# Memory staged by 32 partitions and turned by VectorE, and three quarters of the residual turned through a DRAM scratch issued by ScalarE

## The reference

```python
h = rms_norm(x, norm_mix)
proj = h @ w_in                       # 2048 x 3904: latents of q and kv, rope key, q, k, v of the second head group
q  = rms_norm(c_q,  norm_q_lat)  @ w_q_b
kv = rms_norm(c_kv, norm_kv_lat) @ w_kv_b
o_mla = mla_attention(...)            # 8 heads, causal softmax
o_sb  = stick_breaking_attention(...) # 8 heads
mixed = concatenate([rms_norm(o_mla, norm_mla_out), rms_norm(o_sb, norm_sb_out)])
x = x + mixed @ w_out                 # 2048 x 2048
mem_n = rms_norm(mem, norm_mem_src)
x = x + memory_cross_attention(rms_norm(x, norm_mem_x), mem_n, w_mem_q, w_mem_kv, w_mem_o)
x = x + hierarchical_moe(rms_norm(x, norm_ffn), ...)   # 32 experts, 12 MB of weights each, top 2 of 8 in one of 4 groups
return rms_norm(x, norm_final)
```

## Time and profile before

| | us |
|---|---|
| median of the three runs | 1350.66 |
| lowest and highest | 1350.59, 1352.66 |
| the profiled execution | 1350.58 |
| span of its profile | 1348.8 |
| PE busy in the span | 992.5 |
| DVE busy | 576.0 |
| ACT busy | 303.9 |
| POOL busy | 40.9 |
| bytes moved by DMA | 486.40 MB |

### The profile page before, as it was taken

The page is one execution under the profiler, slowest core; times in us unless marked ns, Lnnn a source line. Parts: engine busy times, 40 slices in busy tenths (PEclk is TensorE's granted clock), DMA queues, the critical chain, the costliest instruction groups (busy, mean ns, idle before and its releaser), DMA issues.

```text
span 1348.8 us, 20643 instructions
## 1 busy us (share of the span) xinstructions
PE 992.5 (74%) x8516; PEld 595.7 (44%) x8516; DVE 576.0 (43%) x1132; ACT 303.9 (23%) x537; POOL 40.9 (3%) x92
## 2 busy tenths in 40 slices
PE   8999999999999975666555666655566655566656
PEld 7888898888888522222222222212222222222222
DVE  5555567776656643233322233332223332223324
ACT  5554457774544100000000000000000000000002
POOL 1300000130000000000000000000000000000001
PEclk9999999999999997778777778787787787777878
DMA  7777764447869999999999999999999999999997
GB/s 245 262 243 250 214 176 125 152 150 276 290 235 354 359 432 429 434 431 432 430 432 434 430 430 430 434 431 430 430 435 431 431 431 431 434 431 430 430 427 307
DMA packets 78021, 486.40 MB, mean 361 GB/s; under 512 B 9944, under 2 KB 25438, under 8 KB 64799
## 3 DMA queue, kind: packets, MB, share of 16 engines
q1 hardware_dynamic: 77484, 483.46, 89.0%
q10 hardware_dynamic: 306, 2.11, 0.4%
q0 software_dynamic: 192, 0.31, 0.2%
HBM read 481.14 MB, written 4.72 MB: 360 GB/s over the span
## 4 chain that ended last, share of the span: by engine, by line
PE 50%; DMA 46%; SPq 1%; DVE 1%; issue 1%; ACT 0%; DVEq 0%; ACTq 0%
DMA gu<-in_w_up 42%; PE ps L1053 10%; PE ps L606 8%; PE ps L608 8%; PE ps L607 8%; PE ps L1108 5%; DMA down<-in_w_down 4%; PE ps L1032 2%; PE ps L1065 1%; PE ps L586 1%; PE ps L851 1%; PE ps L852 1%; PE ps L853 1%; PE ps L778 1%; SPq L471 0%
## 5 line engine op out<-in xcount | busy, mean ns | idle before, releaser
L1053 PE MATMUL ps<-gu,xe 128*32 128x256 f32 x3968 | 284.9, 450 | 305.8 <-DMA gu<-in_w_up 305.3
L2144 DVE TENSOR_TENSOR x_sum<-ps,x_sum 128x512 f32<-128x512 f32 x240 | 149.1, 684 | 508.3 <-PE ps L1065 508.3
L1053 PEld LDWEIGHTS ps<-gu,xe 128*32 128x32 f32 x3968 | 139.7, 129 | 468.9 <-DMA gu<-in_w_up 328.5
L1619 DVE TENSOR_TENSOR w_lo<-w_raw,w_hi 128x1024 fp32r<-128x1024 f32 (+1 forms) x137 | 164.6, 1207 | 117.7 <-ACT w_hi L1226 114.2
L606 PE MATMUL ps<-w_hi,a_hi 128*128 128x512 f32 (+1 forms) x468 | 183.3, 392 | 0.0
L607 PE MATMUL ps<-w_lo,a_hi 128*128 128x512 f32 (+1 forms) x468 | 179.8, 384 | 0.0
L608 PE MATMUL ps<-w_hi,a_lo 128*128 128x512 f32 (+1 forms) x460 | 176.8, 384 | 0.0
L1226 ACT ACTIVATE w_hi<-w_raw 128x1024 fp32r<-128x1024 f32 (+1 forms) x137 | 141.9, 1040 | 128.7 <-PE ps L608 98.2
L1538 ACT ACTIVATE sg<-ps 128x128 f32<-128x128 f32 x31 | 8.6, 278 | 654.3 <-PE ps L1053 654.3
L1108 PE MATMUL ps<-down,act_t 128*32 128x512 f32 x976 | 112.4, 601 | 6.1 <-DMA down<-in_w_down 6.1
L607 PEld LDWEIGHTS ps<-w_lo,a_hi 128*128 128x128 f32 x468 | 88.0, 188 | 16.4
(11 more groups left out here) (335 smaller groups left out, 831.6 us busy)
## 6 DMA issues: line engine op xcount, KB each, us to landing
down<-in_w_down SPq DMA_DIRECT2D x29, 4096.0 KB, 22.7
gu<-in_w_gate SPq DMA_DIRECT2D x28, 4096.0 KB, 31.7
gu<-in_w_up SPq DMA_DIRECT2D x28, 4096.0 KB, 40.9
w_raw<-in_w_in SPq DMA_DIRECT2D x56, 512.0 KB, 5.1
w_raw<-in_w_out SPq DMA_DIRECT2D x32, 512.0 KB, 4.4
gu<-in_w_up SPq DMA_DIRECT2D x18, 512.0 KB, 6.1
w_raw<-in_w_mem_kv SPq DMA_DIRECT2D x16, 512.0 KB, 3.5
down<-in_w_down SPq DMA_DIRECT2D x13, 512.0 KB, 15.2
```

The source lines that it names most:

```text
L1053: mm = pe.matmul(ps[5][j * SLOTS:(j + 1) * SLOTS, 0:2 * P].rearrange("s (m f) -> s m f", m=2), xe[:, k, :], gu[side][:, :, k, j * P:(j + 1 ...
L1619: ve.tensor_tensor(w_lo[:, u % RING, :, 0:n], w_raw[:, u % RING, :, 0:n], w_hi[:, u % RING, :, 0:n], ALU.subtract).then_inc(S("w_split"), 1)
L2144: ins = ve.tensor_tensor(x_sum[:, t, cols], ps[g][:, :], (x_res if first else x_sum)[:, t, cols], ALU.add)
```

## The change

**Memory.** It is loaded by SP in eight pieces of 256 KB during `w_in` (unit numbers in `MEM_AT`), so that 32 tokens lie on 32 partitions for each quarter of the width (`mem_quads`, 128 partitions = 4 quarters x 32 places). ACT takes the squares in eight instructions over 512 elements; DVE turns blocks of 32x32 in eight STREAM_TRANSPOSEs (`turn_mem`). The read skips so that each partition holds 16 *consecutive* rows of the width; therefore the rows of `w_mem_kv` are loaded in the matching order, "(p k)". POOL spreads the squares over a pattern of identities (`mem_spread`), and PE sums them with two matmuls of one column. In the latent stage ACT and DVE round and split from SBUF (`mem_heads`, `mem_rest`), and PE's 8 groups of transposes are gone.

**Residual.** For the first three quarters, ACT issues a write of the quarter to `spill` within the next even chunk (`spill_x`), and two roundings later, after a wait for the landing, four reads into `nat` (`read_x`). In the odd chunk DVE turns it with one STREAM_TRANSPOSE (`memx_turn`), ACT rounds four slices from SBUF and takes the squares, and DVE makes the rests. The fourth quarter is turned by PE as before. The first six units of `w_mem_q` are loaded in the matching row order. SP gets one more wait, for the third turn, ahead of a load of expert weights into that memory.

**Beside them.** Columns of `g_t` are renumbered, and two gains are loaded in their new order directly.

The core of the diff:

```diff
+MEM_AT = [START[_c] + 3 + _q for _c in (SB_Q + 1, SB_V) for _q in range(NJ)]
+X_QUADS = 3
+X_MOVED = len(QUADS)
...
+        mem_quads = place("mem_quads", [P, NJ, UN], offset=v_mla_at)
+        mem_t = place("mem_t", [P, KD, TT * NJ, QUAD], offset=o_at)
...
+        x_quads = nat[:, 0].rearrange("p t (j f) -> p (t j) f", f=P)
+        x_t = nat[:, 1].rearrange("p t (k j s) -> p (t k) j s", k=UK, s=QUAD)
...
 # SP
                 if u == last_units:
+                    sp.wait_ge(S("quads_turned"), X_MOVED + X_QUADS)
                     load_piece(1, 1, 8, 10)
...
+                if u in MEM_AT:
+                    t, q = divmod(MEM_AT.index(u), NJ)
+                    if q == 0:
+                        sp.wait_ge(*((S("squared"), 3 * TT) if t == 0 else (S("mem_turned"), 1)))
+                    sp.dma_start(mem_quads[q * QUAD:(q + 1) * QUAD, :, :],
+                                 mem[0, t * P:(t + 1) * P, q * UN:(q + 1) * UN].rearrange(
+                                     "(j s) f -> s j f", s=QUAD)).then_inc(S("mem_loaded"), 16)
...
 # PE
-            pe.wait_ge(S("mem_loaded"), 16)
+            pe.wait_ge(S("mem_spread"), 1)
+            for t in range(TT):
+                mm = pe.matmul(ps[7][:, t:t + 1], mem_spread[:, NJ * t:NJ * (t + 1), :].rearrange(
+                    "p j s -> p (j s)"), ones[:, 0:1], start=True, stop=True)
+            mm.then_inc(S("squares_summed"), 1)
             for n, (c, i) in enumerate(LATENT):
...
-                if n < KD // 2:
-                    split_turn("mem", mem_sb, 2 * n, 2 * n + 2)
...
             for q in range(1, D // UN):
                 project(W_OUT + 2 * q)
-                pe.wait_ge(*chunk_out(W_OUT + 2 * q - 1))
-                if q == 1:
-                    pe.wait_ge(S("sums_made"), 1)
-                split_turn("memx", x_res, 4 * (q - 1), 4 * q)
                 project(W_OUT + 2 * q + 1, a0=HEADS)
 
             pe.wait_ge(S("split_lo"), SPLIT0["memx"] + KD - 4)
             project_units(MEM_Q, range(0, 3), 0, a2_hi, a2_lo)
...
 # ACT
+            def spill_x(q):
+
+                sc.wait_ge(*chunk_out(W_OUT + 2 * q + 1))
+                sc.dma_start(spill[X_MOVED + q].rearrange("(t p) f -> p t f", p=P),
+                             x_res[:, :, q * UN:(q + 1) * UN]).then_inc(S("spilled"), 16)
+
+            def read_x(q):
+
+                sc.wait_ge(S("spilled"), 16 * (X_MOVED + q + 1))
+                sc.wait_ge(S("quads_turned"), X_MOVED + q)
+                for i in range(NJ):
+                    sc.dma_start(x_quads[i * QUAD:(i + 1) * QUAD, :, :],
+                                 spill[X_MOVED + q, :, i * P:(i + 1) * P].rearrange("(j s) f -> s j f", s=QUAD)
+                                 ).then_inc(S("quads_loaded"), 16)
+
             for c in range(W_OUT, MEM_Q):
+                q, g = divmod(c - W_OUT, 2)
+                if q >= 1:
+                    rounded(START[c] + 1 + RING)
+                    if g == 0:
+                        spill_x(q - 1)
+                        rounded(START[c] + 3 + RING)
+                        read_x(q - 1)
+                    else:
+                        memx_heads(q - 1)
                 rounded(DONE[c] + RING)
-                if c > W_OUT and (c - W_OUT) % 2 == 0:
-                    memx_heads((c - W_OUT) // 2 - 1)
...
 # DVE
+            def turn_mem(t):
+
+                ve.wait_ge(S("squared"), 3 * TT + NJ * (t + 1))
+                for j in range(NJ):
+                    ins = ve.transpose(mem_t[:, :, NJ * t + j, :],
+                                       mem_quads[:, j, :].rearrange("p (r k) -> p k r", k=KD))
+                ins.then_inc(S("mem_turned"), 1)
...
+                if c in (SB_K, SB_V + 1):
+                    split_w(START[c] + RING + 3)
+                    turn_mem((SB_K, SB_V + 1).index(c))
...
+            def memx_turn(q):
+
+                ve.wait_ge(S("quads_loaded"), 16 * NJ * (X_MOVED + q + 1))
+                if q >= 1:
+                    ve.wait_ge(S("split_lo"), SPLIT0["memx"] + 4 * q)
+                ve.transpose(x_t, x_quads.rearrange("p j (r k) -> p k j r", k=NJ)).then_inc(
+                    S("quads_turned"), 1)
...
             for c in range(W_OUT, MEM_Q):
+                q, g = divmod(c - W_OUT, 2)
+                if q >= 1 and g:
+                    split_w(START[c] + 1 + RING)
+                    memx_turn(q - 1)
+                    split_w(START[c] + 2 + RING)
+                    memx_rests(q - 1)
                 split_w(DONE[c] + RING - (1 if c == W_OUT else 0))
                 add_heads(c)
-                if c > W_OUT and (c - W_OUT) % 2 == 0:
-                    memx_rests((c - W_OUT) // 2 - 1)
```

More of the change, by code:

```diff
@@ L113 @@
         _b = len(SPLIT_BANK)
-        SPLIT_BANK.append(6 + _b % 2 if _name == "mem" else 4 + _b % 4)
+        SPLIT_BANK.append(None if _name == "mem" or _name == "memx" and _i < UK * X_QUADS else 4 + _b % 4)
 def bank_before(b):
@@ L198, in layer @@
         kpe_t = place("kpe_t", [P, 2, SEQ])
+        v_mla_at = at[0]
         v_mla = place("v_mla", [P, TT, HEADS * HD])
@@ L308, in unit_src @@
                 return [w_out[0, rows, q * UN:(q + 1) * UN].rearrange("(k p) n -> p k n", p=P)]
+            if c == MEM_Q and i < UK * X_QUADS:
+                q, b = divmod(i, UK)
+                return [w_mem_q[0, q * UN:(q + 1) * UN, :].rearrange(
+                    "(p k) n -> p k n", k=NJ)[:, b * UK:(b + 1) * UK, :]]
             if c == MEM_Q:
@@ L1353, in _, with mem_heads @@
                     chunk_copy(c, lambda t: v_sb[:, t, n0:n0 + UN], SS_X)
+                if c in (SB_Q + 1, SB_V):
+                    mem_squares((SB_Q + 1, SB_V).index(c))
                 if c == SB_K:
[L1355 removed]
+                    split_head("q", 32, hi=cq_hi)
                 if c == SB_K + 1:
[L1357 to L1362 removed]
+                    split_head("kv", 36, hi=ckv_hi)
+            def mem_heads(k):
+                if k == 0:
+                    sc.wait_ge(S("w_used"), START[Q_PE])
+                    sc.wait_ge(S("mem_turned"), TT)
+                sc.activation(a_hi[:, k, :], mem_t[:, k].rearrange("p j s -> p (j s)"), ACT.Copy,
+                              scale=g_t[:, 70 + k:71 + k]).then_inc(S("split_hi"), 1)
             for n, (c, i) in enumerate(LATENT):
@@ L1751, in _, with mem_rest @@
             copy_turned(KV_LAT)
+            def mem_rest(k):
+                ve.wait_ge(S("split_hi"), SPLIT0["mem"] + k + 1)
+                ve.scalar_tensor_tensor(
+                    out=a_lo[:, k, :], in0=mem_t[:, k].rearrange("p j s -> p (j s)"),
+                    scalar=g_t[:, 70 + k:71 + k], in1=a_hi[:, k, :], op0=ALU.mult, op1=ALU.subtract).then_inc(S("split_lo"), 1)
+            ve.sem_inc(S("split_turned"), KD // 2)
+            ve.wait_ge(S("squares_summed"), 1)
+            ve.tensor_copy(sums[:, SS_MEM:SS_MEM + TT], ps[7][:, 0:TT]).then_inc(S("sums_made"), 1)
             for n, (c, i) in enumerate(LATENT):
@@ L2329, in _ @@
             scale_latent(c_kv, KV_RANK, SS_KV, 3)
+            for q in range(1, NJ):
+                link(gp.tensor_tensor(quad_eye[:, :], ident[:, 0:QUAD] if q == 1 else quad_eye[:, :],
+                                      ident[:, q * QUAD:(q + 1) * QUAD], ALU.add))
+            gp.wait_ge(S("squared"), 3 * TT + TT * NJ)
+            gp.tensor_tensor(
+                mem_spread[:, :, :],
+                quad_eye[:, :].rearrange("p (a s) -> p a s", a=1).to_broadcast([P, TT * NJ, QUAD]),
+                chunk_ss[:, :, :].rearrange("p t j -> p (t j)").rearrange(
+                    "p (j a) -> p j a", a=1).to_broadcast([P, TT * NJ, QUAD]),
+                ALU.mult).then_inc(S("mem_spread"), 1)
+            norms([SS_MEM], D, "sums_made", 1)
             def add_squares(h):
```

109 lines of the change are left out of this document (63 added, 46 removed).

## The result

The changed kernel takes 1374.39 us (median of 5 runs, 1372.08 to 1375.12) against 1351.84 us (5 runs): 1.0167 of the time before, 95% interval 1.0156 to 1.0178, 22.5 us slower. The forecast was 1354.2 with a range up to 1360.0: the sign was right, the size far off. The profiled executions are 1373.77 us (span 1372.0) and 1350.58 us (span 1348.8), 23.2 us apart.

The account below looks back on a forecast made before the run. PE was taken to bound the dense part and expert-weight loads the expert stage, which moves with it. 1350.6 - 3.35 (memory) + 5.4 (residual loop) + 1.5 (clock) = 1354.2 us, range 1348.5 to 1360.

Parts of the forecast that it names:

- What bounds the kernel: PE bounds the dense layers to about 445 us, expert-weight loads the stage behind, which moves with it one for one.
- The memory part, -3.35 us: Latent stage: removing 8 groups of transposes from PE gains 3.35 us net; new turns and squares are hidden in w_in.
- The residual as a loop against PE's 21.8 us: W_out stretch: first pass 20.7 us, then loops of 24.4 against PE's 21.8; first memory-query unit 5.4 us later.
- Their landing is hidden if it takes less than ... 4.8 us.: Residual loop: the four reads' landing adds nothing if shorter than the 4.8 us of steps up to the turn.
- The 3 MB of traffic: W_out stretch: spills and reads need 9 us of all DMA engines, 14 us are free in 70; costed at nothing.
- The write, 6.2 us: Residual loop: a spill takes 6.2 us from issue to landing, bounds 5.0 and 8.1.
- The turn, 1.16 us: Residual loop: DVE's transpose of a quarter adds 1.16 us, from old turns of the same 1024 elements at 1.24.
- the rival of the slow turn: Residual loop: strided SBUF reads make each of three turns 1.2 us longer, giving 1357.9 us; chance 0.20.
- PE's rest: PE stands still once, before the first memory-query unit, about 8 us less small earlier waits on w_lo.
- The clock, +1.5: After its rest before the memory queries PE resumes at the 1.2 GHz level, costing 1.35 us, rounded up to 1.5.
- Another issuer makes the transfer no quicker: Residual spills: issuers share the same 16 DMA engines, so with ACT instead of SP the landing stays 6.2 us.
- The range: Whole time: 1348.5 us (spill at 5.0, no clock loss) to 1360 (spill at 8.1 or a slow turn).

Follow-up runs that it names:

- the run with long runs: Changed kernel with each of the four reads taking the same 128 KB in runs of 4 KB instead of 512 bytes; 1373.45 us in one run.

## Why the prediction was wrong

- **What bounds the kernel**: right. The expert stage moved one for one (23.26 and 23.2 us).
- **The memory part, -3.35 us**: right, -3.03. Its turns took 1.035 us each instead of 0.72 and were hidden.
- **The residual as a loop against PE's 21.8 us**: the mechanism was right, and so was the place of the last wait. The size was not. From the first addition to the first rests were 26.5 us against 20.7, and the two loops behind took 30.1 and 31.7 against 24.4 (rests ending at 338.0, 368.1, 399.8). That is 18.8 us more in three passes, and with the 0.7 us that the clock cost more than forecast behind the last stop it is nearly the whole miss: 1373.8 in the profiled execution against 1354.2.
- **The step that failed: "Their landing is hidden if it takes less than ... 4.8 us."** From the start of the reads' issue to the turn the sum allowed 1.83 + 4.8 = 6.6 us; measured were 10.3, 9.5 and 12.2 us, 12.1 of the 18.8 us. The landing got no number and no row: it was called hidden. The chain in order of time, the last read of the first and of the third pass:

```profile
320.20 8.90 DMA nat<-spill
380.13 10.80 DMA nat<-spill
```

  The old reads could not have served as a measure. SP issues them behind its wait for the write, so no fresh load stands ahead of them. The changed kernel still has them, beside the new ones, in one execution; they land in 2.6 us, and the new ones in 7.1 (above). DMA issues up to 560 us:

```profile
nat<-spill SPq DMA_DIRECT2D x4, 128.0 KB, 2.6
```

- **The 3 MB of traffic, costed at nothing because 20% of the DMA engines was free over 70 us**: on that average the bytes fit, but the transfers ran in windows in which the engines were 94 to 106% busy, from 341.64 to 359.21 and from 371.72 to 390.93. The share to read was that of the moment, not of the stretch.
- **The write, 6.2 us**: 7.2, 8.1 and 7.0, 3.8 us more in the three passes. Its upper bound of 8.1, from a row with much in flight, was nearer.
- **The turn, 1.16 us**: 1.985. This was the rival of the slow turn, to which 0.20 had been given; it was true, and worth 0.75 us in each loop (1.2 had been estimated). The row was at hand: the turn from PSUM with a stride took 717 ns, which was read as no more than a plain one by size, yet half of the plain 1236 is 618. The Trainium skill, "Advanced Engine Details and Errata", section "SBUF Cachelines", says that accesses which go to a new 16-byte line each time are penalised; the two turns of 1024 elements (1.985 and 1.245 us) agree.
- In the loop from 341.64 these are 1.9 + 2.9 + 0.8 = 5.6 of the 5.7 us by which it is longer than forecast.
- **PE's rest, "once", about 8 us less small waits**: three rests, 23.2 us. The chain had ACT's roundings in it, so the loop also sets the pace of the *weights*, and PE stopped for them in the first and the second loop. The chain sets the sum of the rests; how it is shared out among them doesn't change the end.
- **The clock, +1.5**: 2.2 us behind the last rest. The other two rests had their price too (1.3 and 1.8), but off the chain.
- **Another issuer makes the transfer no quicker**: right. 2.8 us with SP and 2.8 with ACT when alone. What the prediction cites from the Trainium skill, "DMA: Bandwidth & Descriptors", section "Issuing engines are not separate DMA queues", agrees with both runs. But the 6.2 us which stood beside it was no property of the transfer.
- **The range**: its upper end of 1360 was a write of 8.1 us in three passes (5.7 us more) *or* a slow turn, never both, and the reads' landing had no bound at all, as it was called hidden.

## What to carry to other kernels

A duration of a transfer is that of its company: before it is used in another place, look at what its queue's issuer did meanwhile, and whether the DMA engines are full at the moment it goes to, which an average over the stage doesn't show. Here that was a factor of 2.5. Where a chain through DMA has room, give each step a stage of its own on an in-order engine, so that its semaphore has come before the engine gets to the wait: the same work went from 1374 to 1345 us by order alone. And in a loop that is longer than its consumer's work an error of one term comes back in each pass, so a term that is called hidden needs a number and a bound as the others do.

## What the runs showed of the hardware

- 512 KB to DRAM landed in 2.8 us almost alone (DMA engines 68% busy) and in 7.0 to 8.1 us beside loads of 512 KB (95 to 102%); 128 KB pieces back in 2.6 to 2.8 and in 7.1 (medians).
- With reads in runs of 4 KB instead of 512 bytes, beside other loads, the turn came 0.8 to 3.0 us sooner behind the first read's issue, of 9.5 to 12.2.
- A STREAM_TRANSPOSE of 128x1024 f32 in SBUF: 1.245 us contiguous, 1.985 us with 16 bytes from element to element; 128x512 with 64 bytes: 1.035 us.
- PE resumed at the 1.2 GHz level after a rest of 4.3 us as after one of 12.2, and each cost 1.3 to 2.2 us more. In the run with long runs, behind a rest of 3.45 us, the first six matmuls still came at full clock (1.00 from 336.9 to 338.2) and the next eight at half (0.50 from 338.6 to 341.5).
